# Two attention layers behind an mLSTM block: the values of the turned pairs multiplied ahead of the next logits

## The chip, the cores and the metric

The kernel runs on one core of a Trainium2 chip. The metric is the time of one execution on the device in microseconds (us), as the median of several runs. Three runs of the kernel before took 1127.65, 1127.94 and 1127.89 us, a median of 1127.89 us.

## The reference, cut to what matters

A hybrid block (pooling and a chunkwise mLSTM) is followed by two attention layers over 512 tokens and 1024 channels. Each layer normalises x, projects it, attends, gates the result with silu(z), and projects it back onto x. The change touches only the attention of both layers:

```
even layer:  6 sliding-window heads with sinks, 6 block-sparse heads
             (two blocks of 256 keys, the past one always selected: causal, with slopes), 4 memory heads
odd layer:   12 forgetting heads (causal, bias from a cumulative sum), 4 memory heads
per head:    s = q @ k.T * scale + bias ; p = softmax(s) ; o = p @ v      (head width 64)
             y = concat(o) * silu(z) ; x = x + y @ w_out
```

## The kernel before, in words

One program text per engine, written out by hand in program order; engines meet at semaphores. Operands of the large products are split into a high and a low part, so that a product is three matmuls (lines 2234 to 2236, helper `product`). The layers are called L = 0 (even) and L = 1 (odd, the last one).

**Pairs.** A layer's 16 heads make 8 head pairs, and each head pair has 4 row tiles of 128 queries in the order t = 0, 3, 1, 2 (`ROW_TILES`): 32 pairs p = 0 to 31. A pair is two jobs (e = 0, 1), one for each head. For the causal heads (pairs 12 to 23 of L = 0, pairs 0 to 23 of L = 1) a job has t + 1 blocks of 128 keys, so the four pairs of a head pair have 1, 4, 2 and 3 blocks. Window heads (pairs 0 to 11 of L = 0) have 1 or 2 blocks, memory heads (pairs 24 to 31) have 2.

**The life of a pair.** TensorE (PE) makes the logits of both jobs in two PSUM banks of `acc` (`logits`, line 2720: tiles of 64 rows by 128 columns, since a head has 64 channels). For forgetting heads two bf16 matmuls of full 128 by 128 tiles add the causal mask on the diagonal (`triangles`, line 2735). VectorE (DVE) adds the bias, takes the row's extreme and writes `pr` (`biased`, line 2054, an instruction and a read of the accumulator for each job; `least_of_pair`, line 2061, for memory heads). ScalarE (ACT) takes the exponentials (line 1415), DVE the reciprocals (line 2034), ACT scales (line 1422). PE transposes `pr` block by block into two banks of `aux` (`turn`, line 2744, full 128 by 128 tiles). DVE copies them to `prT` (`turned`, line 2069). PE multiplies the values (`weighted`, line 2756: two matmuls of 128 by 64 tiles for each block) into `out_bank`. When a head pair's four tiles are through, DVE gates it (`gated_out`, line 2089), ACT takes the high part and DVE the low part (`rest`, line 1531; in line 957 GpSimd, POOL, makes that of other columns).

**The rounds.** PE's text has rounds i = 0 to 17 in each layer (NQ = 16). Round i in the kernel before: logits and triangles of pairs 2i and 2i+1; `weighted` of pairs 2i-4 and 2i-3 (from i = 2 on); `turn` of pair 2i-2; two parts of the z projection; `turn` of pair 2i-1; two more parts of z. A z part is one `product` of 128 by 128 tiles with 512 columns. From round 16 on there are no logits, and terms of the output projection (lines 2669 to 2671) stand in z's place. In every round, `weighted(k)` waits for DVE's copy of pair k, `logits(p)` waits in `banks_free(p)` for what read the bank two pairs earlier, and `turn(k)` waits for ACT's scaled pair and for the copy of the pair before.

**DVE's order in round i** (A = 2i, B = 2i+1): copy of pair A-3; reciprocals of A-1; in even rounds `gate` of z; `biased` of A; in odd rounds from 3 on `gated_out`; copy of A-2; reciprocals of A; `biased` of B; in odd rounds `rest`. So the copy of pair 2i-3, which `weighted(2i-3)` needs in round i, is what DVE does last, behind `rest`, before its work of round i. Its pair has 4 blocks when i is even and the heads are causal (4 blocks are two copies of 512 columns), and 3 blocks when i is odd.

The weights of z come by DMA from SyncE's queue, and POOL splits them in pieces of 512 columns (lines 874 and 875), in its own pace beside the rounds. Rows of the cumulative sum for the forgetting heads come by DMA on SyncE's queue (line 832), each held back until the head three before it is through `biased` of its last tile.

Of the kernel before, what the change touches and what calls it, by code (L numbers as in the profile page):

```python
# [120 lines left out]
def hybrid_block_then_two_attention_layers(nc, A, vecs_d, consts_d, out):  # L121
    stack = ExitStack()
    with stack:
# [271 lines left out]
        more = {plan["e_qk"][0]: 4, plan["e_qk"][0] + 1: 3, plan["e_z"][0]: 4, plan["e_z"][0] + 1: 3}  # L395
        more[plan["e_out"][0]] = 3
        more.update({n: (2, 1, 0, 0, 0, 0, 0)[u] for n, (_, u) in OUT_UNITS.items() if u})

        PROJ = ("pa", "pb")
        MERGED_ORDER = (4, 5, 6, 7, 0, 1, 2, 3)  # L400
        PROJ_UNITS = {plan[name][0] + u: (i, u) for i, name in enumerate(PROJ) for u in range(7)}
        more.update({n: 1 for n, (_, u) in PROJ_UNITS.items() if u in (S3_T3, S2_T2, S1_T1, A22_T4)})

        def loaded(n):
# [39 lines left out]
        for name in ("e_z", "o_z"):  # L444
            BY_POOL.update(range(plan[name][0], plan[name][0] + 4))
        BY_POOL.update(n for n, (_, u) in OUT_UNITS.items() if u < 3)
        STAGED = {n for n, (_, u) in OUT_UNITS.items() if u >= 3}

# [14 lines left out]
        def wait_split(eng, n):  # L463
            if n in STAGED:
                eng.wait_ge(term_w_split, LATE * OUT_UNITS[n][0] + OUT_UNITS[n][1] - 2)
                return
            eng.wait_ge(w_split_pool if n in BY_POOL else w_split, splits(n))
# [1760 lines left out]
        def _(pe):  # L2228
# [328 lines left out]
            for L, name in enumerate("eo"):  # L2557
# [80 lines left out]
                def z_product(i):  # L2638

                    u, half, k = i // (2 * KT), i // KT % 2, i % KT  # L2640
                    n0, a0, _ = plan[name + "_z"]
                    n, a = n0 + u, a0 + u
                    if k == 0 and half == 0:
                        wait_split(pe, n)
                        if u:
                            pe.wait_ge(acc_free, a)
                    if k == 0 and half:
                        pe.wait_ge(z_half, 4 * L + u + 1)
                    c = k * UC + half * P
                    ins = product(z_bank, whi[:, n % SLOTS, c:c + P], wlo[:, n % SLOTS, c:c + P],  # L2650
                                  ht_hi[:, k, :], ht_lo[:, k, :], k == 0, k == KT - 1)
                    if k == KT - 1:
                        ins.then_inc(acc_ready, 1)
# [52 lines left out]
                def logits(p):  # L2706
                    first = pairs[p][0]
                    forget = first.bias is not None and first.bias[0] == "forget"
                    j = p // TT
                    if j >= FIRST_SPLIT:  # L2710
                        query, key = parts_of_pair(L, j)
                        if first.t == ROW_TILES[0]:
                            pe.wait_ge(part_split, max(split_number(L, query), split_number(L, key)))
                        rows = slice(P * first.t, P * first.t + P)
                        keys = slice(P * first.k0, P * first.k0 + first.keys)
                        (q_hi, _, q_lo), (k_hi, _, k_lo) = (split_operand(L, part) for part in (query, key))
                        for n, (q, k) in enumerate(((q_hi, k_hi), (q_hi, k_lo), (q_lo, k_hi))):
                            for e, job in enumerate(pairs[p]):
                                (_, qp), (_, kp) = job.q, job.k
                                ins = mm(logit_bank(L, p, e)[:, 0:first.keys], q[qp:qp + HD2, rows], k[kp:kp + HD2, keys],  # L2720
                                         start=n == 0, stop=n == 2 and not forget)
                        if not forget:
                            ins.then_inc(logit_ready, 1)

                def banks_free(p):

                    if p == 1:
                        pe.wait_ge(acc_free, plan[name + "_z"][1])
                    if p >= 2:
                        pe.wait_ge(nm_ready if pairs[p - 2][0].bias is not None else pr_ready, 2 * (done + p - 1))  # L2730
                def triangles(p):
                    if pairs[p][0].bias is None or pairs[p][0].bias[0] != "forget":
                        return
                    for e, job in enumerate(pairs[p]):
                        ins = mm(logit_bank(L, p, e)[:, job.keys - P:job.keys], ident_b[:], causal_b[:], start=False, stop=True)
                    ins.then_inc(logit_ready, 1)

                def turn(k):
                    if done + k:
                        pe.wait_ge(prT_copied, done + k)  # L2740
                    for e, job in enumerate(pairs[k]):
                        pe.wait_ge(norm_ready, 2 * (done + k) + e + 1)
                        for b in range(job.keys // P):
                            ins = nc.tensor.transpose(trans_bank(e)[:, P * b:P * b + P],  # L2744
                                                      pr[:, pr_slot(k, e), P * b:P * b + P], ident[:])
                    ins.then_inc(prT_ready, 1)

                def weighted(k):
                    pe.wait_ge(prT_copied, done + k + 1)
                    job = pairs[k][0]  # L2750
                    j, nb = k // TT, job.keys // P
                    if job.t == 0 and (L or j):
                        pe.wait_ge(t_ready, 32 + 8 * L + j)
                    for b in range(nb):
                        for e, one in enumerate(pairs[k]):
                            ins = mm(out_bank[HD2 * e:HD2 * e + HD2, P * job.t:P * job.t + P],  # L2756
                                     (mv if job.bias is None else vv)[:, job.k0 + b, one.v:one.v + HD2],
                                     prT[L][2 * (k % 2) + e][:, P * b:P * b + P], start=b == 0, stop=b == nb - 1)
                    ins.then_inc(o_ready, 1)

                for i in range(NQ + 2):
                    if 0 < i < NQ:
                        banks_free(2 * i)
                        banks_free(2 * i + 1)
                        logits(2 * i)
                        logits(2 * i + 1)
                        triangles(2 * i)
                        triangles(2 * i + 1)
                    elif i == 0:
                        banks_free(0)  # L2770
                        logits(0)
                        triangles(0)
                        banks_free(1)
                        logits(1)
                        triangles(1)
                    if i >= 2:
                        weighted(2 * i - 4)
                        weighted(2 * i - 3)
                    if 1 <= i <= NQ:
                        turn(2 * i - 2)  # L2780
                    if i < NQ:
                        z_product(4 * i)
                        z_product(4 * i + 1)
                    if i == NQ:

                        pe.wait_ge(acc_free, a_out)
                        pe.wait_ge(pr_ready, 2 * (done + NP))
                        pe.wait_ge(lo_ready, 32 + 8 * L + 4)
                        wait_split(pe, n_out + A11_B11)
                        for e in range(2):  # L2790
                            term(L, A11_B11, e)
                    if 1 <= i <= NQ:
                        turn(2 * i - 1)
                    if i < NQ:
                        z_product(4 * i + 2)
                        z_product(4 * i + 3)
                    if i == NQ:
                        pe.wait_ge(s3_ready, 4 * SEVEN.index(L) + 4)
                        wait_split(pe, n_out + S3_T3)
                        term(L, S3_T3, 0)  # L2800
# [55 lines left out]
```

## Time and profile before

| | |
|---|---|
| median of 3 runs | 1127.89 us (1127.65 to 1127.94) |
| the profiled execution, its own time | 1128.07 us |
| its span | 1126.2 us |
| PE's share of the chain that ended last | 98% |
| attention rounds of L = 0, first logits to last values | 711.9 to 815.2 us |
| attention rounds of L = 1 | 980.4 to 1092.8 us |
| PE waiting at `weighted` for a copy, L = 1 rounds (waits view) | 0.4 us in one wait |
| DVE waiting for line 2735 in the L = 1 rounds | 10.8 us in 10 waits |

The table is read so: the profiled execution is 0.18 us above the median, and 1.87 us of it lie outside the span. A timeline row gives the start in us from the span's start, the time in us that the merged instructions took, engine, line, operation, what is written and read, shape and count, and in brackets the idle time of the engine just before it with what ended it. A group of PE rows that follow each other without a gap is best read by the distance of their starts: the end of a matmul is modelled, the next start is not. Each matmul of line 2756 stands in the trace as two records, so "x20" there is ten matmuls.

### The profile page before, as it was taken

The numbers are of one execution on the slowest core, as the hardware profiler recorded it, in microseconds if no ns is written. First come the engines' busy times: TensorE is split into PE (matmuls) and PEld (weight loads), VectorE is DVE, ScalarE is ACT, GpSimd is POOL, SyncE is SP. The second block draws the span as 40 slices with busy tenths as digits, with TensorE's granted clock in tenths as the row PEclk, the third lists the DMA queues.
The fourth block names the chain that finished last, engine by engine and source line by source line (L and its number), as shares of the span: only waits on it lengthen the run. The fifth ranks groups of instructions, "written<-read, shape, count | busy, mean of one in ns | idle before, by whom it ended". The sixth has DMA issues, their size and how long they took to land.

```text
span 1126.2 us, 16358 instructions
## 1 busy us (share of the span) xinstructions
PE 1119.9 (99%) x6378; PEld 944.0 (84%) x6378; DVE 750.7 (67%) x1256; ACT 637.3 (57%) x1088; POOL 179.1 (16%) x199
## 2 busy tenths in 40 slices
PE   9999999999999999999999999999999999999998
PEld 7888889888888888889989888777788888877787
DVE  5584746688746776564868667676786575667786
ACT  5533454244436667645447678777545587577742
POOL 1100000111111000000000002644403000606530
PEclk9999999999999999999999999999999999999999
DMA  7893235797897942234547323231344233222432
GB/s 245 266 192 112 76 117 187 243 233 201 237 212 221 204 104 66 80 124 150 187 168 193 107 75 94 58 109 43 120 179 115 88 99 104 75 76 76 154 118 76
DMA packets 117318, 157.25 MB, mean 140 GB/s; under 512 B 18860, under 2 KB 85804, under 8 KB 114680
## 3 DMA queue, kind: packets, MB, share of 16 engines
q1 hardware_dynamic: 103112, 118.45, 33.4%
q0 software_dynamic: 12896, 33.56, 13.0%
q10 hardware_dynamic: 1232, 4.19, 1.0%
q8 instruction: 51, 0.84, 0.3%
q14 instruction: 27, 0.22, 0.1%
HBM read 151.83 MB, written 37.90 MB: 168 GB/s over the span
## 4 chain that ended last, share of the span: by engine, by line
PE 98%; ACT 1%; DMA 1%; DVE 0%; issue 0%; SPq 0%; DVEq 0%
PE acc L2234 19%; PE acc L2236 19%; PE acc L2235 19%; PE aux L2234 3%; PE aux L2236 3%; PE aux L2235 3%; PE aux L2756 3%; PE aux L2744 3%; PE acc L2720 3%; PE acc L2435 2%; PE acc L2436 2%; PE acc L2434 2%; PE acc L2669 2%; PE acc L2670 2%; PE acc L2671 2%; PE aux L2502 1%
## 5 line engine op out<-in xcount | busy, mean ns | idle before, releaser
L2234 PE MATMUL acc<-ht_hi,whi 128*128 128x512 f32 x712 | 278.0, 390 | 0.0
L2236 PE MATMUL acc<-ht_hi,wlo 128*128 128x512 f32 x712 | 277.1, 389 | 0.0
L2235 PE MATMUL acc<-ht_lo,whi 128*128 128x512 f32 x712 | 277.1, 389 | 0.0
L1492 DVE TENSOR_TENSOR wlo<-raw,whi 128x2048 fp32r<-128x2048 f32 x74 | 169.4, 2289 | 100.9 <-ACT whi L1011 97.0
L1011 ACT ACTIVATE whi<-raw 128x2048 fp32r<-128x2048 f32 x74 | 141.4, 1911 | 61.0 <-DMA raw<-w_in_dram 18.4
L2236 PEld LDWEIGHTS acc<-ht_hi,wlo 128*128 128x128 f32 x712 | 133.7, 188 | 27.8
L2234 PEld LDWEIGHTS acc<-ht_hi,whi 128*128 128x128 f32 x712 | 133.7, 188 | 27.6 <-DVE wlo L1492 0.2
L2235 PEld LDWEIGHTS acc<-ht_lo,whi 128*128 128x128 f32 x712 | 133.7, 188 | 27.2
L874 POOL TENSOR_SCALAR whi<-raw 128x512 fp32r<-128x512 f32 x52 | 39.2, 754 | 473.4 <-DMA raw<-e_w_in_dram 314.8
L2234 PE MATMUL acc<-whi,ht_hi 128*128 128x512 f32 (+1 forms) x224 | 84.0, 375 | 0.0
L2236 PE MATMUL acc<-whi,ht_lo 128*128 128x512 f32 (+1 forms) x224 | 83.8, 374 | 0.0
L2235 PE MATMUL acc<-wlo,ht_hi 128*128 128x512 f32 (+1 forms) x224 | 83.7, 374 | 0.0
L1422 ACT ACTIVATE pr<-pr,stats 128x256 f32<-128x256 f32 (+3 forms) x128 | 61.2, 526 | 20.8 <-DVE stats L2034 20.0
L875 POOL TENSOR_TENSOR wlo<-raw,whi 128x512 fp32r<-128x512 f32 x52 | 69.6, 1338 | 4.3
L2069 DVE COPY prT<-aux 128x256 f32<-128x256 f32 (+3 forms) x128 | 52.1, 448 | 17.4 <-PE aux L2744 17.4
L1415 ACT ACTIVATE pr<-pr,stats 128x257 f32<-128x257 f32 (+5 forms) x96 | 51.1, 534 | 8.1 <-DVE stats L2054 7.1
L2234 PE MATMUL aux<-ht_hi,whi 128*128 128x512 f32 x128 | 55.6, 435 | 0.0
L2236 PE MATMUL aux<-ht_hi,wlo 128*128 128x512 f32 x128 | 50.6, 395 | 0.0
L2235 PE MATMUL aux<-ht_lo,whi 128*128 128x512 f32 x128 | 50.0, 390 | 0.0
L1723 DVE SCALAR_TENSOR_TENSOR cacc<-cpad,vecs,cacc 128x512 f32<-128x512 f32 x64 | 48.1, 752 | 2.3
L2236 PEld LDWEIGHTS acc<-whi,ht_lo 128*128 128x128 f32 x224 | 42.2, 188 | 7.5
L2235 PEld LDWEIGHTS acc<-wlo,ht_hi 128*128 128x128 f32 x224 | 42.2, 188 | 7.4
(415 smaller groups left out, 2313.0 us busy)
## 6 DMA issues: line engine op xcount, KB each, us to landing
raw<-w_in_dram SPq DMA_DIRECT2D x72, 512.0 KB, 4.8
raw<-o_w_in_dram SPq DMA_DIRECT2D x28, 512.0 KB, 4.7
raw<-weight_terms SPq DMA_DIRECT2D x10, 1024.0 KB, 4.8
weight_terms<-weight_terms POOLq DMA_DIRECT2D x8, 1024.0 KB, 9.4
raw<-e_w_in_dram SPq DMA_DIRECT2D x14, 512.0 KB, 5.1
weight_terms<-w_proj_pool_dram POOLq DMA_DIRECT2D x6, 1024.0 KB, 7.3
weight_terms<-w_proj_mlstm_dram POOLq DMA_DIRECT2D x6, 1024.0 KB, 6.5
weight_terms<-o_w_out_dram POOLq DMA_DIRECT2D x6, 1024.0 KB, 6.9
```

Of the source, the lines that this page charges most:

```text
L874: step(nc.gpsimd.tensor_scalar(whi[:, slot, piece], source[:, piece], 1.0, 1.0, ALU.mult, ALU.mult))
L875: ins = nc.gpsimd.tensor_tensor(wlo[:, slot, piece], source[:, piece], whi[:, slot, piece].bitcast(F32), ALU.subtract)
L1011: nc.scalar.activation(whi[:, slot, :], raw[:, slot, :], ACT.Copy).then_inc(w_hi, 1)
L1415: nc.scalar.activation(tile, tile if job.bias is not None else logit_bank(L, p, e)[:, 0:job.keys], ACT.Exp, scale=-1.0, bias=stats[:, 1, i ...
L1422: nc.scalar.activation(tile, tile, ACT.Copy, scale=stats[:, 4, 2 * p + e:2 * p + e + 1]).then_inc(norm_ready, 1)
L1492: v.tensor_tensor(wlo[:, slot, :], raw[:, slot, :], whi[:, slot, :].bitcast(F32), ALU.subtract).then_inc(w_split, 1)
L1723: ins = v.scalar_tensor_tensor(out_, cpad[:, slot, k:k + S], V("conv_w", j * TAPS + k), out_, ALU.mult, ALU.add)
L2069: ins = v.tensor_copy(prT[L][2 * (k % 2) + e][:, 0:job.keys], trans_bank(e)[:, 0:job.keys])
L2234: mm(out_, w_hi_, x_hi, start=first, stop=False)
L2235: mm(out_, w_hi_, x_lo, start=False, stop=False)
L2236: return mm(out_, w_lo_, x_hi, start=False, stop=last)
L2720: ins = mm(logit_bank(L, p, e)[:, 0:first.keys], q[qp:qp + HD2, rows], k[kp:kp + HD2, keys], start=n == 0, stop=n == 2 and not forget)
```

## The change

In each round from 2 on, the two `weighted` calls stand at the head of PE's round and not behind the logits and triangles. Nothing else is changed: the same instructions, the same waits on the same semaphores, and the texts of the other engines stay. Rounds 0 and 1 have no `weighted`, and rounds 16 and 17 have no logits, so that the order differs in rounds 2 to 15 of both layers, 28 rounds in all.

```diff
--- before.py
+++ after.py
@@ -2759,6 +2759,9 @@
                     ins.then_inc(o_ready, 1)
 
                 for i in range(NQ + 2):
+                    if i >= 2:
+                        weighted(2 * i - 4)
+                        weighted(2 * i - 3)
                     if 0 < i < NQ:
                         banks_free(2 * i)
                         banks_free(2 * i + 1)
@@ -2773,9 +2776,6 @@
                         banks_free(1)
                         logits(1)
                         triangles(1)
-                    if i >= 2:
-                        weighted(2 * i - 4)
-                        weighted(2 * i - 3)
                     if 1 <= i <= NQ:
                         turn(2 * i - 2)
                     if i < NQ:
```

## Rows read from the trace of the kernel before

**Rows 1.** The page's part 1: busy time, share of the span and instructions of each engine.

```profile
PE 1119.9 (99%) x6378; PEld 944.0 (84%) x6378; DVE 750.7 (67%) x1256; ACT 637.3 (57%) x1088; POOL 179.1 (16%) x199
```

**Rows 2.** Timeline of PE, last layer, rounds 9 and 10: start, us, engine, line, operation, [idle].

```profile
1037.32 0.39 PE L2236 MATMUL aux<-ht_hi,wlo 128*128 128x512 f32 x1
1037.63 0.39 PE L2720 MATMUL acc<-op_lo,op_hi 64*128 64x256 f32 x2
...
1038.72 0.40 PE L2735 MATMUL acc<-causal_b,ident_b 128*128 128x128 bf16 x4
1039.04 1.31 PE L2756 MATMUL aux<-prT,v_o 128*64 128x128 f32 x20
1040.29 0.44 PE L2744 MATMUL aux<-ident,pr 128*128 128x128 f32 x2
1040.48 0.47 PE L2234 MATMUL aux<-ht_hi,whi 128*128 128x512 f32 x1
...
1044.30 0.33 PE L2720 MATMUL acc<-op_lo,op_hi 64*128 64x128 f32 x2
```

**Rows 3.** Timeline of PE, round 1 of the last layer (no values yet).

```profile
986.15 0.40 PE L2735 MATMUL acc<-causal_b,ident_b 128*128 128x128 bf16 x4
986.38 0.39 PE L2744 MATMUL aux<-ident,pr 128*128 128x128 f32 x2
986.52 0.48 PE L2234 MATMUL aux<-ht_hi,whi 128*128 128x512 f32 x1
```

**Rows 4.** Timeline of PE, round 16 of the layer before: values right behind z.

```profile
803.50 0.40 PE L2236 MATMUL aux<-ht_hi,wlo 128*128 128x512 f32 x1
803.83 1.09 PE L2756 MATMUL aux<-prT,mv 128*64 128x128 f32 x16
```

**Rows 5.** Timeline of DVE, round 9 of the last layer.

```profile
1039.84 0.08 DVE L2054 DVE_READ_ACCUMULATOR2_ANT stats<- 128x1 f32 x1
1040.40 0.69 DVE L2089 SCALAR_TENSOR_TENSOR qk_o<-aux,zT 128x512 f32<-128x512 f32 x1 [0.48 <-PE aux L2756]
...
1042.42 0.42 DVE L1531 TENSOR_TENSOR op_lo<-qk_o,op_hi 128x256 fp32r<-128x256 f32 x1
1043.02 1.29 DVE L2069 COPY prT<-aux 128x512 f32<-128x512 f32 x2 [0.18 <-PE aux L2744]
```

**Rows 6.** Timeline of DVE, round 10 of the last layer: the first copy.

```profile
1047.80 0.76 DVE L2069 COPY prT<-aux 128x256 f32<-128x256 f32 x2 [1.33 <-PE aux L2744]
```

**Rows 7.** Timelines of DVE, POOL and PE, round 5 of the last layer.

```profile
1015.33 1.29 POOL L875 TENSOR_TENSOR wlo<-raw,whi 128x512 fp32r<-128x512 f32 x1
1015.44 1.46 DVE L1531 TENSOR_TENSOR op_lo<-qk_o,op_hi 128x256 fp32r<-128x256 f32 x1
...
1016.83 1.28 DVE L2069 COPY prT<-aux 128x512 f32<-128x512 f32 x2
...
1017.33 0.33 PE L2720 MATMUL acc<-op_lo,op_hi 64*128 64x128 f32 x2
```

**Rows 8.** Timelines of DVE and PE, rounds 7 and 11 of the last layer.

```profile
1029.77 1.28 DVE L2069 COPY prT<-aux 128x512 f32<-128x512 f32 x2
...
1030.82 0.33 PE L2720 MATMUL acc<-op_lo,op_hi 64*128 64x128 f32 x2
...
1056.65 1.27 DVE L2069 COPY prT<-aux 128x512 f32<-128x512 f32 x2
...
1057.80 0.39 PE L2720 MATMUL acc<-op_lo,op_hi 64*128 64x256 f32 x2
```

**Rows 9.** Timelines of DVE and PE, round 11 of the layer before.

```profile
776.34 0.69 DVE L2089 SCALAR_TENSOR_TENSOR qk_e<-aux,zT 128x512 f32<-128x512 f32 x1 [0.89 <-PE aux L2756]
...
778.96 1.28 DVE L2069 COPY prT<-aux 128x512 f32<-128x512 f32 x2
...
780.23 0.39 PE L2720 MATMUL acc<-op_lo,op_hi 64*128 64x256 f32 x2
```

**Rows 10.** DMA issues: the rows of the cumulative sum, KB each, us to landing.

```profile
csum_all<-csum_rows SPq DMA_DIRECT2D x12, 256.0 KB, 3.6
```

## The prediction

> **What bounds the kernel now.** I read the page's part 1 first. TensorE is busy 1119.9 of 1126.2 us [rows 1], so a reordering can gain only what lies between its instructions, and each wait it adds on TensorE is paid in full unless a later wait swallows it; with 6.3 us not busy in the whole span there is hardly one that could. Then TensorE's timeline of one round of the last layer [rows 2]: z, logits, the causal matmuls (line 2735), the values (ten matmuls, x20 as two records each, 1.25 us from start to start), the transposes. The reader is to see that no wait stands in it: each group starts 0.2 to 0.33 us behind the last start of the one before. Then VectorE's timeline of the same round [rows 5]: it idles 0.48 us until the values are done, gates, copies, biases, makes the rest, and last copies the four-block pair, in 1.29 us. That copy ends at 1044.31, and TensorE's next round starts at 1044.30 [rows 2]. Today the logits stand between the start of the round and the values that need this copy. The change takes that cover away.
>
> **What it removes and adds.** Nothing is added or dropped in count. A measurement of this kernel can tell about 0.2%, 2.26 us, from no change.
>
> *Changes of tile shape.* In a round of the last layer with forgetting heads TensorE goes from full tiles (z) to 64-row tiles (logits), to full (causal), to 64-column (values), to full (transposes): four changes. After the edit it goes z, values, logits, causal, transposes: the causal matmuls and the transposes are both full tiles, so three changes. What that is worth is seen in round 1 of that layer, where the transposes already follow the causal matmuls: 0.23 us from the causal start to the transposes and 0.14 for two transposes to z [rows 3], against 0.32 from the causal start to the values and 0.19 for two transposes to z [rows 2]. The saving is 0.32 + 0.19 - 0.23 - 0.14 = 0.14 us a round. It holds in rounds 2 to 11 of the last layer, ten rounds: 1.4 us. In the other 18 rounds there are three changes before and after, and I cost them at nothing. The step from z to the values is seen where no logits are left: 0.33 us [rows 4], against 0.31 from z to the logits [rows 2]; at most 0.02 a round, 0.6 us over 28.
>
> The Trainium skill, "TensorEngine Tiling (Array Packing)", Key Properties, says that changing the tiling mode drains the engine; the steps just read agree with it, and counting changes alone it would make this edit a gain of those ten rounds and nothing else.
>
> *Values straight to logits.* The trace never shows this step. One change of shape costs about 0.09 us by the causal rows (0.32 against 0.23). From below, the step costs nothing; from above, twice as much. I take 0.09, since it is one change of shape as the others are; the ends are 28 x 0.09 = 2.5 us to either side.
>
> *The wait for the copy.* `weighted(2i-3)` now starts when the first pair's values are done. In an even round that is one block of five, 0.25 of the 1.25 us [rows 2]; so the copy of the four-block pair must be there 0.25 us into the round. In odd rounds the pair has three blocks and two blocks of values stand ahead, and I find no wait. Next, how late does the copy come? In the odd round ahead, the logits come 1.25 us later, since the values go first, so `biased` of pair A starts that much later. `gated_out` stood idle 0.48 us for the values [rows 5]; they are now early, so it follows `biased` at once (0.08 us beside the accumulator's read) and comes 1.25 - 0.48 - 0.08 = 0.69 us later. Everything on VectorE behind it moves with it, but for the 0.18 us in which the copy stood idle [rows 5]: 0.51 us.
> - Rounds 4 and 10 (round 3 is like round 9): the copy ends at 1044.31 + 0.51 = 1044.82; it is wanted at 1044.30 - 0.14 + 0.25 = 1044.41. Wait 0.41 each, 0.8 together.
> - Round 6: here the copy is late already, because `rest` (line 1531) took 1.46 us instead of 0.42 beside a GpSimd instruction [rows 5, 7]. Wanted at 1017.33 - 0.14 + 0.25 = 1017.44. If `rest` is as long again, the copy ends at 1016.83 + 0.69 + 1.28 = 1018.80, wait 1.36. If it takes 0.42, it ends at 1017.83, wait 0.39. GpSimd's instruction ended at 1015.33 + 1.29 = 1016.62 and the copy began at 1016.83; if it again begins there, it ends at 1018.11, wait 0.67. I take 0.7.
> - Round 8: 1029.77 + 0.69 + 1.28 = 1031.74 against 1030.93 [rows 8], wait 0.81; with a short `rest` 0.36; I take 0.5.
> - Round 12: 1056.65 + 0.69 + 1.27 = 1058.61 against 1057.91 [rows 8], wait 0.70; low end 0.6; I take 0.7.
> - Round 2 has no delayed round before it. In the layer before, `gated_out` idled 0.89 us [rows 9], so VectorE is only 1.25 - 0.89 - 0.08 = 0.28 late: round 12 there has its copy at 778.96 + 0.28 + 1.28 = 780.52, wanted at 780.23 + 0.25 = 780.48. All of that layer: 0.1.
>
> Sum 0.8 + 0.7 + 0.5 + 0.7 + 0.1 = 2.8 us, between 2.3 and 3.8.
>
> For round 6 the Trainium skill, "SBUF — State Buffer", Who interferes with whom, says that a VectorE instruction with two inputs in SBUF is blocked fully until a GpSimd instruction that reads SBUF ends. By it the three long cases go to 0.67, 0.36 and 0.6, the waits to 2.5, and the total below to 1129.0; row and rule agree in round 5, where `rest` ended soon after GpSimd did.
>
> *What else is moved.* The wait in `banks_free` comes later, so it can only shrink; no row shows it as a wait now. Behind a waiting `weighted` on TensorE stand the logits, and behind those VectorE's `biased`; but in even rounds VectorE waits 1.33 us for the transposes [rows 6] and `biased` of a one-block pair is short, so the lateness doesn't add up from round to round. Reciprocals, exponentials and scalings come about 0.7 to 1.25 us later in odd rounds; the transposes want them a round, over 6 us, later [rows 2]. SyncE's queue: the rows of the cumulative sum wait for `biased`, so they go out about 0.7 us later and take 3.6 us [rows 10]; their reader is later by 1.25 us. The z weights depend on z parts, which follow TensorE. GpSimd waits for no logits. I cost these at nothing; if that cover went, the price would be of the kind of VectorE's 0.7 us.
>
> **Sum.** -1.4 + 2.8 = +1.4 us. The profiled execution took 1128.07, so 1129.5; it stands 0.18 us above the median of the runs, so 1129.3 for the median, +0.12%: no change that can be told.
>
> **Rivals.**
> *A, slower: the copies come later than that.* Place: VectorE between `gated_out` and the four-block copy, in rounds 5, 7 and 11 of the last layer, where GpSimd splits weights. If `rest` stands as long each time as in round 5, rounds 6, 8 and 12 wait 1.36 us each: 0.8 + 4.1 + 0.1 = 5.0, less 1.4 is +3.6, 1131.5. It decides from 3.7 us of waits on. For it: all of it was seen once [rows 7]. Against: rounds 7 and 11 were milder [rows 8], and GpSimd's own instruction ends the hold.
> *B, no waits: only the saved change of shape is left.* -1.4, 1126.5. It needs VectorE to be some 0.5 us earlier than I count in every odd round. For it: the margins are tenths of a microsecond. Against: in round 6 the copy ends at 1018.11 even without any delay, 0.67 us after it is wanted [rows 7].
> *C, values to logits is dearer:* 2.5 us more, 1131.8. For: never seen. Against: every change of shape that is seen costs alike.
> *D, it is free:* 2.5 us less, 1126.8; with B at once 1124.0, the only way to a gain of over 0.2%.
> *E, nothing moves:* TensorE was held by something else and the new order is hidden; 1127.9. Against: it is busy 99%.
>
> **How the numbers follow.** My forecast with its bounds 0.50; A 0.17; B 0.12; C 0.10; D 0.05 (with B 0.04 more); E 0.02. The range reaches from D to C, 1126.8 to 1131.8, takes in A's centre and leaves out B's point and the far ends, about 2 in 10. Faster by over 0.2% (below 1125.6): D with B and the tail of B, 0.06. Slower (above 1130.15): A, C and the upper part of my own case, whose 3.8 us of waits come to +2.4: 0.17 + 0.10 + 0.05 = 0.32. Within: 0.62.
>
> **What would show it.** Right: waits of TensorE at line 2756 for line 2069 in rounds 4, 6, 8, 10 and 12 of the last layer, 0.4 to 0.8 us each, and hardly any in the layer before; the causal matmuls to the transposes in 0.23 us in ten rounds; VectorE's idle time ahead of `gated_out` gone; odd rounds of the last layer shorter by 0.14 us. Wrong: even rounds as short as before (B); all 28 rounds longer or shorter by a tenth (C, D); waits over 1 us behind a long `rest` (A); or a wait of TensorE at the transposes, which would say that the later logits do reach a round further.

## The result and the profile after

The changed kernel takes 1130.5 us in the median of 8 runs (1129.93 to 1132.62), the kernel before 1127.68 (1127.48 to 1128.11) in the runs beside them: +2.8 us, ratio 1.0025 (95% interval 1.0015 to 1.0034). The profiled execution took 1130.38 us with a span of 1128.6; its span is 2.4 us longer than that of the kernel before.

The page's part 1 of the changed kernel answers to [rows 1]; TensorE (PE) is as busy as ever, since a short wait between two groups is hardly seen there:

```profile
PE 1121.0 (99%) x6378; PEld 942.5 (84%) x6378; DVE 749.0 (66%) x1256; ACT 635.2 (56%) x1088; POOL 179.0 (16%) x199
```

The waits view of the changed kernel over the last layer's rounds says more (engine and line, what it waited for, us in total, times, longest):

```profile
DVE pr L2054 <- PE acc L2735: 23.0, 11, 2.7
...
PEld aux L2744 <- DVE prT L2069: 3.9, 7, 0.7
...
PEld aux L2756 <- DVE prT L2069: 3.5, 10, 0.4
...
PE aux L2744 <- DVE prT L2069: 1.3, 5, 0.3
```

VectorE (DVE) waits 23.0 us for the causal matmuls, 10.8 before, and the idle time ahead of line 2089 is gone from the list. New is a wait at line 2744, the transposes, for the copies. The weight load's waits (PEld) need care: one stands at every change of tile shape, whatever it is put down to (0.36 or 0.37 us from z to the values, 0.17 from the values to the logits, 0.25 or 0.36 from the logits to the causal matmuls), and is no wait for another engine by itself. The steps of the timeline decide. Round 9 of the last layer in the changed kernel, TensorE:

```profile
1039.14 1.31 PE L2756 MATMUL aux<-prT,v_o 128*64 128x128 f32 x20
1040.38 0.38 PE L2720 MATMUL acc<-op_lo,op_hi 64*128 64x256 f32 x2
...
1041.46 0.40 PE L2735 MATMUL acc<-causal_b,ident_b 128*128 128x128 bf16 x4
1041.69 0.39 PE L2744 MATMUL aux<-ident,pr 128*128 128x128 f32 x2
1041.84 0.47 PE L2234 MATMUL aux<-ht_hi,whi 128*128 128x512 f32 x1
...
1043.72 1.09 PE L2744 MATMUL aux<-ident,pr 128*128 128x128 f32 x8 [0.25 <-DVE prT L2069]
...
1046.14 1.31 PE L2756 MATMUL aux<-prT,v_o 128*64 128x128 f32 x20
```

and VectorE in the same round:

```profile
1041.89 0.43 DVE L2054 CUSTOM_DVE_ANT_0 pr<-acc,csum_all 128x256 f32<-128x256 f32 x1 [2.72 <-PE acc L2735]
...
1042.59 0.69 DVE L2089 SCALAR_TENSOR_TENSOR qk_o<-aux,zT 128x512 f32<-128x512 f32 x1
1043.19 0.48 DVE L2069 COPY prT<-aux 128x128 f32<-128x128 f32 x2
...
1044.60 0.42 DVE L1531 TENSOR_TENSOR op_lo<-qk_o,op_hi 128x256 fp32r<-128x256 f32 x1
1044.93 1.28 DVE L2069 COPY prT<-aux 128x512 f32<-128x512 f32 x2
```

The reader is to see four things against [rows 2, 3, 5]. From the causal matmuls to the transposes it is now 0.23 us, and from these to z 0.15: the saving is there. Gating starts 3.45 us into the round, 2.77 before: 0.68 later, as forecast (0.69). Behind it stands the copy of the first pair, pair 2i-2. It ends at 1043.67, and at 1043.72 the transposes of the second pair begin, 1.88 us behind the z group and not 1.47: TensorE waited 0.41 us, and the eight transposes that follow take 0.85 us from start to start instead of 0.79. That is 0.47 us in all, and it was not in my sum. And the four-block copy ends at 1046.21, while the next round, late by that wait, wants it at 1046.14 + 0.25: no wait there.

Read so for all 32 rounds (steps from the start of one group to the next, profiled executions):

| | before | changed | difference |
|---|---|---|---|
| L = 0, first logits to the values of round 16 | 91.95 us | 92.57 us | +0.62 |
| of it transposes of rounds 3 and 5 | | 2 x 0.21 | +0.42 |
| of it values of round 12 | 1.24 us | 1.36 us | +0.12 |
| L = 1, the same | 101.02 us | 102.90 us | +1.88 |
| of it changes of shape, rounds 2 to 11 | | 10 x -0.14 | -1.4 |
| of it transposes of rounds 3, 5, 7, 9, 11 | | 5 x 0.47 | +2.35 |
| of it values of rounds 6, 8, 12 | 1.24, 1.25, 1.25 us | 1.53, 1.47, 1.58 us | +0.84 |

The two layers give +2.5 us, the span +2.4. The rest of both rows is a few hundredths in single steps. Odd rounds 3 to 11 of the last layer are 0.33 or 0.34 us longer, where the prediction had them 0.14 shorter; even rounds 4 and 10, for which it had waits, are 0.14 to 0.16 shorter.

### The profile page after: what moved, and what is told of

Read it like the earlier page. It is cut to its first block, busy times and chain, and to the rows that moved or that the text cites. A ratio compares the mean times of both kernels' runs of the same rounds, so it can differ in the third digit from the quotient of the medians.

```text
span 1128.6 us, 16358 instructions
## 1 busy us (share of the span) xinstructions
PE 1121.0 (99%) x6378; PEld 942.5 (84%) x6378; DVE 749.0 (66%) x1256; ACT 635.2 (56%) x1088; POOL 179.0 (16%) x199
## 4 chain that ended last, share of the span: by engine, by line
PE 97%; DVE 1%; ACT 1%; issue 0%; DMA 0%; DVEq 0%; ACTq 0%
PE acc L2234 19%; PE acc L2236 19%; PE acc L2235 19%; PE aux L2756 3%; PE aux L2234 3%; PE aux L2236 3%; PE aux L2235 3%; PE acc L2720 3%; PE aux L2744 3%; PE acc L2435 2%; PE acc L2436 2%; PE acc L2434 2%; PE acc L2669 2%; PE acc L2671 2%; PE acc L2670 2%; PE aux L2502 1%
## 5 line engine op out<-in xcount | busy, mean ns | idle before, releaser
L2234 PEld LDWEIGHTS acc<-whi,ht_hi 128*128 128x128 f32 x224 | 42.2, 188 | 7.7 <-issue 0.3
```

The costliest lines, as they stand in the source:

```text
L2234: mm(out_, w_hi_, x_hi, start=first, stop=False)
```

## The experiments

Theory 1 (from the trace after): two waits for copies, one at the second pair's transposes and one at the values, less the saved changes of shape. The first comes from this chain: logits 1.25 us later, `biased` of the first pair, gating, copy of pair 2i-2; `turn(2i-1)` waits for that copy, since both pairs are transposed into the same banks. Theory 2 is the prediction's: the wait at the values alone. Each median is of 11 runs (5 for "copy ahead of gating") and is compared with that of the kernel before on the same chip.

| run | median | against before | ratio, 95% interval | L = 0 rounds | L = 1 rounds |
|---|---|---|---|---|---|
| odd rounds alone | 1130.16 | +2.2 | 1.0020 (1.0011 to 1.0028) | +0.54 | +1.81 |
| even rounds alone | 1127.58 | -0.35 | 0.9995 (0.9985 to 1.0004) | +0.03 | -0.19 |
| last layer alone | 1129.90 | +2.0 | 1.0015 (1.0007 to 1.0024) | 0 | +2.98 |
| copy ahead of gating | 1132.07 | +4.1 | 1.0033 (1.0020 to 1.0046) | +0.63 | +2.94 |
| low part later | 1129.28 | +1.4 | 1.0015 (1.0006 to 1.0024) | +0.46 | +0.96 |
| both edits | 1127.71 | -0.2 | 0.9999 (0.9990 to 1.0007) | +0.11 | -1.16 |
| even rounds, low part later | 1127.22 | -0.7 | 0.9993 (0.9984 to 1.0002) | +0.03 | -0.78 |
| kernel before, both edits | 1129.96 | +2.1 | 1.0018 (1.0009 to 1.0027) | +0.70 | +0.70 |
| both edits, low part behind the gate | 1127.84 | +0.1 | 0.9999 (0.9991 to 1.0008) | +0.29 | -1.08 |
| causal matmuls last | 1128.96 | +1.2 | 1.0011 (1.0002 to 1.0021) | 0 | +0.97 |
| the same, copy ahead of gating | 1126.97 | -0.8 | 0.9992 (0.9983 to 1.0001) | 0 | -1.07 |
| the same, low part later too | 1126.48 | -1.4 | 0.9991 (0.9982 to 1.0000) | 0 | -1.39 |

The last two columns are rounds 0 to 15 of one profiled execution against those of the kernel before. Steps that no wait touches agree to hundredths between these executions; waits for a copy can differ from one execution to another. One case stands apart: the profiled execution of the last layer alone was among its slowest (1130.59), and its last layer took 1.1 us more than the same text took in the changed kernel's profile.

**Odd or even rounds.**

```diff
 for i in range(NQ + 2):
+    values_first = i % 2 == 1      # the other run: i % 2 == 0
+    if i >= 2 and values_first:
         weighted(2 * i - 4); weighted(2 * i - 3)
...
+    if i >= 2 and not values_first:
+        weighted(2 * i - 4); weighted(2 * i - 3)
     if 1 <= i <= NQ: turn(2 * i - 2)
```

> Values ahead of the logits in odd rounds alone, both layers. Theory 1 (the trace of the changed kernel: TensorE waits at the transposes of the second pair, line 2744, because VectorE's copy of the first pair stands behind a bias and a gating that come 1.25 us later): five waits of 0.47 us in odd rounds 3 to 11 of the last layer, two of 0.21 in rounds 3 and 5 of the layer before, less five saved changes of shape of 0.14: +2.1 us against the kernel before, about 1129.8. No wait at the values (line 2756), since in even rounds the logits cover the late copy again. Theory 2 (the prediction's: the only price is the wait at the values for the four-block copy): no waits at all, -0.7 us, 1127.0.

> Values ahead of the logits in even rounds alone, both layers. Theory 1: VectorE is not delayed in odd rounds, so no wait at line 2744; at line 2756 only what was late in the kernel before already: up to 0.7 us in round 6 of the last layer, 0.1 in round 8, less 0.7 saved changes of shape: between -0.6 and +0.2 us, 1127.1 to 1127.9. If instead the values ahead of the logits cost something by themselves in every round, half of the change's 2.8 us would be here: +1.4, 1129.1.

Measured: +2.2 and -0.35 us. The timeline of the run with odd rounds alone has the wait at line 2744, here in round 9 of the last layer:

```profile
1041.46 0.39 PE L2744 MATMUL aux<-ident,pr 128*128 128x128 f32 x2
1043.49 1.09 PE L2744 MATMUL aux<-ident,pr 128*128 128x128 f32 x8 [0.25 <-DVE prT L2069]
```

The five rounds each took 7.01 us (6.67 before), and no values waited; round 13 of each layer, with memory heads, was 0.08 or 0.09 longer: there the logits of round 14 waited for ScalarE's exponentials, which read the logits' banks (in the last layer the read ended at 1071.86 and the logits began at 1071.95). In the changed kernel the values stand between, and that wait, which the prediction had priced at nothing in `banks_free`, is not there. In the run with even rounds alone no transposes waited; values took 1.59 us in round 6 and 1.40 in round 12 of the last layer (1.24 and 1.25 before), and the other four changed rounds of that layer with forgetting heads were 0.13 to 0.16 shorter. Theory 2's -0.7 for the odd rounds is refuted: most of the change's cost lies in the odd rounds' late logits.

**The last layer alone** (`values_first = L == 1`).

> The change in the last layer alone. Theory 1: five waits at the transposes (2.35 us), three at the values (0.8), ten saved changes of shape (-1.4): +1.8 us, 1129.5. A price that every changed round pays alike would put half of 2.8 here: +1.4.

Measured +2.0, with ten saved changes of shape and five waits of 0.47 at the transposes. Its profiled execution shows a third thing, the length that the wait at the values can have. Round 8, VectorE, GpSimd (POOL) and TensorE:

```profile
1030.19 1.29 POOL L875 TENSOR_TENSOR wlo<-raw,whi 128x512 fp32r<-128x512 f32 x1
1030.29 1.48 DVE L1531 TENSOR_TENSOR op_lo<-qk_o,op_hi 128x256 fp32r<-128x256 f32 x1
...
1031.69 1.28 DVE L2069 COPY prT<-aux 128x512 f32<-128x512 f32 x2
...
1031.84 0.44 PE L2756 MATMUL aux<-prT,v_o 128*64 128x128 f32 x4
...
1033.02 1.09 PE L2756 MATMUL aux<-prT,v_o 128*64 128x128 f32 x16 [0.74 <-DVE prT L2069]
```

The low part stood behind GpSimd's instruction (1.48 us for 0.42) and put 0.96 us on the values, where the changed kernel's own profile had 0.22 behind a low part of 0.74 us. Round 6 of this run has the same on a smaller scale: a low part of 1.32 us and 0.79 us on the values, 0.29 in the changed kernel's profile. It may be a reason for the spread of the changed kernel's runs, 2.7 us against 0.6 before. But the kernel before went up to 1129.92 itself in later runs, and I have no profile of the changed kernel's slowest, so that stays open.

**VectorE's order: copy ahead of gating.**

```diff
-if out_due(i) is not None: gated_out(out_due(i))
 if 1 <= i <= NQ: turned(A - 2)
+if out_due(i) is not None: gated_out(out_due(i))
```

> The changed kernel, and on VectorE the copy of pair 2i-2 stands ahead of the gating in odd rounds. Theory 1: the waits at line 2744 go (0.47 in five rounds, 0.21 in two). TensorE comes to the next even round earlier by as much, and the four-block copy does not come earlier, so the waits at line 2756 grow to what the prediction gave, 0.4 to 0.8 us in rounds 4, 6, 8, 10 and 12 of the last layer, 2.7 in all: about +1.4 us against the kernel before, 1129.1, that is 1.4 less than the changed kernel. If the waits at the transposes had another cause than this order, they stay and the time is that of the changed kernel, 1130.5.

Measured +4.1 against before; the forecast was +1.4. Its first half held. The transposes of round 9 follow at once (1.47 us of z), and the values wait instead, here in round 10:

```profile
1042.20 0.39 PE L2744 MATMUL aux<-ident,pr 128*128 128x128 f32 x2
1043.81 1.03 PE L2744 MATMUL aux<-ident,pr 128*128 128x128 f32 x8
1046.15 0.44 PE L2756 MATMUL aux<-prT,v_o 128*64 128x128 f32 x4
1047.01 1.09 PE L2756 MATMUL aux<-prT,v_o 128*64 128x128 f32 x16 [0.42 <-DVE prT L2069]
```

The values' steps in the last layer were 1.65, 1.81, 2.42, 1.88, 1.90 us in rounds 4 to 12 and 1.93 in round 14: waits of 0.41, 0.57, 1.18, 0.64, 0.66 and 0.90. My prediction had 0.41, 0.7, 0.5, 0.41, 0.7 for the first five, 2.7 us, and 3.5 came, inside its 2.3 to 3.8; most of the excess is round 8, where the low part stood 1.22 us beside a GpSimd instruction. So its wait is real, and in the changed kernel it is mostly hidden, because the wait at the transposes has already made TensorE late. What I had not expected: three waits of 0.14 to 0.21 in the layer before, the wait of 0.90 in the last layer's round 14 (behind a late gating and a low part of 1.70 us), and 0.4 us more in round 16 of both layers (see below).

**The low part later**, alone and with the copy moved.

```diff
 if 2 <= i: turned(A - 3)
+if out_due(i - 1) is not None and i <= NQ:
+    j, cols = out_due(i - 1), y_cols(L, out_due(i - 1))
+    rest(y_tile(L, j)[:, cols], op_hi[:, j, cols], op_lo[:, j, cols])
...
-rest(y_tile(L, j)[:, cols], op_hi[:, j, cols], op_lo[:, j, cols])
+if j == KT - 1: rest(y_tile(L, j)[:, cols], op_hi[:, j, cols], op_lo[:, j, cols])
```

> The changed kernel, and on VectorE the low part of the gated output (line 1531) of an odd round stands behind the four-block copy, at the head of the next round, instead of before it. Theory 1 (two separate waits): the waits at the values (line 2756) go, 0.9 us; the five of 0.47 and two of 0.21 us at the transposes (line 2744) stay: 1129.6. Rival (one wait that moves: any lateness of VectorE finds TensorE somewhere): the time stays at 1130.3 or more.

> The changed kernel with both edits on VectorE: the copy ahead of the gating, and the low part behind the four-block copy. Theory 1: neither wait is left, the ten saved changes of shape are: 1127.9 - 1.4 = 1126.5, up to 0.3 more in rounds where GpSimd holds VectorE. Rival: VectorE is simply too full in odd rounds once the logits come 1.25 us later, and a wait comes back at line 2756: 1128 to 1130.

Measured +1.4 and -0.2. With the low part moved alone the values' steps that had waits are 1.24 or 1.25 us again and the five 0.47 and two 0.21 waits stand as before: the two waits can be taken away singly. With both moved, the last layer's rounds are 1.16 us shorter than before the change; five waits of 0.04 to 0.07 at the values are left. Yet only 0.2 us of it arrives. The rest goes at the first term of the output projection in round 16, where the step from the transposes is 0.83 and 0.85 us in place of 0.45 in the two layers.

**Three checks.**

> Values ahead of the logits in even rounds alone, and the low part behind the four-block copy. Theory 1: the two waits at line 2756 of the run with even rounds alone (0.35 in round 6, 0.15 in round 12 of the last layer) go, five saved changes of shape stay: 1127.9 - 0.7 = 1127.2.

> Control: the kernel before, with both edits on VectorE. TensorE waits for nothing there, so both theories expect no difference: 1127.9, within 0.3. If it is faster, the gain of the run with both edits isn't the change's.

> The changed kernel with both edits on VectorE, and the low part behind the gate of z and not ahead of it. Theory 1: the two waits of 0.38 us at the first term of the output projection in round 16 of both layers, which the run with both edits shows, go: 1127.7 - 0.8 = 1126.9, 1.0 us faster than the kernel before.

The first came out as expected, 1127.22. The other two failed. The control is 2.1 us slower, so the edit on VectorE has costs of its own that have nothing to do with the change. Its waits view over the layer before (last layer the same) shows two:

```profile
PEld acc L2724 <- ACT pr L1415: 1.4, 2, 1.0
PE acc L2724 <- ACT pr L1415: 0.6, 1, 0.6
PEld acc L2673 <- DVE zT L2075: 0.4, 1, 0.4
```

(Its lines 2724 and 2673 are 2720 and 2669.) The logits of round 14 come 0.70 us late, behind the exponentials of memory heads, which read the logits' banks themselves; and the term of round 16 comes 0.39 or 0.40 late. In both layers together that is 2.2 us. With the low part put behind the gate,

```diff
-if 2 <= i: turned(A - 3); (low part of round i-1)
+if 2 <= i: turned(A - 3)
...
 if z_due(i) is not None: gate(z_due(i))
+(low part of round i-1)
```

the term is still 0.84 us behind the transposes (and in round 6 of the layer before the transposes waited 0.21, for a copy behind a low part of 1.10 us that now stood ahead of it). The third run's timeline of ScalarE (ACT), VectorE and TensorE shows why:

```profile
1078.98 0.63 ACT L1050 ACTIVATE op_hi<-qk_o 128x512 fp32r<-128x512 f32 x1 [0.51 <-DVE qk_o L2089]
1079.52 0.89 ACT L1422 ACTIVATE pr<-pr,stats 128x256 f32<-128x256 f32 x2
1080.32 0.46 ACT L1415 ACTIVATE pr<-acc,stats 128x256 f32<-128x256 f32 x1
...
1081.21 0.59 ACT L1396 ACTIVATE zT<-aux 128x512 f32<-128x512 f32 x1
...
1081.84 0.69 DVE L2075 SCALAR_TENSOR_TENSOR zT<-zT,aux 128x512 f32<-128x512 f32 x1 [0.32 <-ACT zT L1396]
...
1082.58 0.50 PE L2673 MATMUL acc<-whi,op_hi 128*128 128x512 f32 x1 [0.18 <-DVE zT L2075]
```

It is not the low part. The gating, now behind the copy, is late, ScalarE waits for it at the head of its queue, and its exponentials and the tanh of z are late behind it. The two single edits show it: with the low part later alone the step is 0.46 us in both layers, with the copy ahead of the gating alone 0.83 and 0.85. I had blamed the wrong one of two edits.

**The causal matmuls last, logits first.** If the saving is the change of shape alone, the values need not go ahead of the logits at all:

```diff
     logits(2 * i); logits(2 * i + 1)
-    triangles(2 * i); triangles(2 * i + 1)
...
 weighted(2 * i - 4); weighted(2 * i - 3)
+triangles(2 * i); triangles(2 * i + 1)
 turn(2 * i - 2)
```

> The kernel before, and only the causal matmuls (line 2735) stand behind the values and ahead of the transposes; the logits stay ahead of the values. Theory 1: the ten saved changes of shape are had (-1.4), the copies at line 2756 stay covered by the logits (no wait), but VectorE gets the forgetting heads' logits 1.25 us later as in the changed kernel, so the five waits of 0.47 us at line 2744 in the last layer are here (+2.35) and the two of the layer before are not: +0.9 us against the kernel before, 1128.8. If the waits at the transposes came from the place of the values and not from the late bias, they would be gone: -1.4, 1126.5.

> As the run before, and on VectorE the copy stands ahead of the gating in the last layer's rounds 0 to 11 alone, so that the memory heads' rounds are as before (there the same edit cost 0.7 us a layer in the control). Theory 1: no wait at line 2744 nor 2756, the changes of shape saved: 1127.9 - 1.4 = 1126.5. Rival: VectorE's lateness finds another wait, time at or above the kernel before.

> The run with the causal matmuls behind the values and the copy ahead of the gating in rounds 0 to 11 of the last layer, and besides the low part (line 1531) behind the four-block copy. In the run without it TensorE waited 0.38 us at the values of round 12, behind a low part that was late. Theory 1: this wait goes, the ten saved changes of shape stay: 1.4 us below the kernel before, 1126.4. Rival: the low part ahead of the reciprocals makes another engine late: 1127 or more.

Measured +1.2, -0.8 and -1.4; in the last two the copy is moved in rounds 0 to 11 of the last layer alone. The first has the saving and the five waits at the transposes, none at the values (round 9):

```profile
1039.07 1.31 PE L2756 MATMUL aux<-prT,v_o 128*64 128x128 f32 x20
1040.32 0.40 PE L2735 MATMUL acc<-causal_b,ident_b 128*128 128x128 bf16 x4
1040.55 0.39 PE L2744 MATMUL aux<-ident,pr 128*128 128x128 f32 x2
1042.58 1.09 PE L2744 MATMUL aux<-ident,pr 128*128 128x128 f32 x8 [0.24 <-DVE prT L2069]
```

The second is free of the wait at the transposes and keeps one of 0.38 at the values of round 12. The third has neither: every round 2 to 11 of the last layer takes 0.13 to 0.15 us less than before, 1.39 in all, and the median is 1126.48 against 1127.9. Its round 9 (lines 2763, 2742 and 2751 are 2756, 2735 and 2744), where the next transposes follow 1.48 us behind the z group:

```profile
1037.58 1.31 PE L2763 MATMUL aux<-prT,v_o 128*64 128x128 f32 x20
1038.82 0.40 PE L2742 MATMUL acc<-causal_b,ident_b 128*128 128x128 bf16 x4
1039.06 0.39 PE L2751 MATMUL aux<-ident,pr 128*128 128x128 f32 x2
1039.20 0.48 PE L2241 MATMUL aux<-ht_hi,whi 128*128 128x512 f32 x1
...
1040.68 0.49 PE L2751 MATMUL aux<-ident,pr 128*128 128x128 f32 x3
```

It is the only version that had all of the gain (-1.4 us); its interval ends at 1.0000, so the runs' medians alone hardly tell it from the kernel before, while its profile does.

## Why the prediction was right or wrong

The range (1126.8 to 1131.8) held the result and the sign was right, but the sum of +1.4 us is half of the 2.8 that came; "no change that can be told" was the likeliest case and the result lies just above that bound. That the time lies inside the range is partly luck: 2.8 us of waits that the sum did not have stand in it, and 1.8 us of those that it had are missing, by the same cause. Of the signs listed, two of the right ones failed (waits at line 2756 in all five even rounds, odd rounds shorter by 0.14), and one of the wrong ones came: a wait of TensorE at the transposes. It came in the same round, though, and not a round further, as the prediction read it.

- *Changes of shape*, -1.4: right, ten rounds of 0.13 to 0.15, and shown by themselves in the last of the runs with the causal matmuls last. The Trainium skill, "TensorEngine Tiling (Array Packing)", Key Properties, says that a change of tiling mode drains TensorE; the trace agrees in that the step into each new shape costs 0.09 to 0.10 us more and the step without a change nothing; it does not show what the engine does in that time.
- *Values to logits*, 0: right. The step costs what values to transposes costs; the changed kernel's rounds with three changes of shape before and after are, but for the waits in the table, equal to those before within 0.03. Rivals C and D fell.
- *Gating 0.69 us later*: right, 0.68.
- *The wait at the values*, 2.7 us in five rounds of the last layer and 0.1 in the layer before: mis-sized for this kernel, 0.84 us in three rounds and 0.12 in one. The mechanism is shown by the run with the copy moved, 3.5 us in the same five rounds. In the changed kernel the next line hides it.
- *The step that failed* is "Everything on VectorE behind it moves with it", which I followed only to the four-block copy. Between lies the copy of pair 2i-2, and `turn(2i-1)` waits for it; the text of the program says so, and I had written it down. It costs 5 x 0.47 + 2 x 0.21 = 2.8 us. I then looked for waits at the transposes only through ScalarE's scaled pair ("a round, over 6 us, later"), not through the shared banks.
- *Rival A*, long waits behind a held `rest`: not in the changed kernel's profile, but seen in the run with the last layer alone, 0.79 and 0.96 us in rounds 6 and 8, and with the copy moved, 1.18 us in round 8. What the prediction cites from the Trainium skill, "SBUF — State Buffer", Who interferes with whom, that a VectorE instruction with two inputs in SBUF is blocked until the GpSimd instruction ends, agrees: in round 7 of the run with the last layer alone the copy began 1031.69 - 1031.48 = 0.21 us behind the end of GpSimd's instruction, the same 0.21 as in [rows 7].
- *Rival B*, no waits: it did not come. Another kernel, with the logits first and both edits, has no waits and takes 1126.48, where I had put B at 1126.5.
- *Rival E*, nothing moves: it did not come; each added wait arrived in the time (+2.5 us of steps, +2.4 of span).

## What to carry to other kernels

When a producer is moved back, list every semaphore of each instruction behind its consumer, not only of the one whose lateness you looked for; a bank shared by two pairs is such a wait. Two late events on one engine are not added: the first wait gives the second its slack, and taking the first away can bring the second back (0.84 us of waits at the last layer's values became 4.4). And look for what a reorder really saves: here it was one change of tile shape, which could be had without moving the values ahead of the logits.

## What the runs showed of the hardware

A change of TensorE's tile shape costs 0.09 to 0.10 us here at the step into the new group, in every pairing that occurs, also between fp32 and bf16 groups. An fp32 group then takes 0.05 us more over its first step (two transposes to z: 0.19 us behind the values, 0.14 or 0.15 behind the causal matmuls), so that one change less in a round saved 0.14. Two neighbouring groups of one shape but different type (causal bf16, transposes fp32) cost none. A TensorE wait of 0.4 us costs 0.47: the eight transposes behind it took 0.85 us from start to start, 0.79 without the wait.
